# One decoder block on one core: sums on VectorE in two recurrent rounds, another order of the jobs around attention, another place for one expert load, and a shorter end

## The reference

```python
proj = xn @ w_in                      # u | q | k | v | q_idx | k_idx | w_idx | g_ssm | g_att
y_ssm = s5_mixer(u, ...)              # scan of 32 groups x 64 complex states, gelu, GLU
y_att = dsa_attention(q, k, v, q_idx, k_idx, w_idx)   # 64 best keys of 256 by 16 index heads
mixed = g_ssm * (y_ssm @ w_proj_ssm) + g_att * (y_att @ w_proj_attn)
x = x + mixed @ w_out
x = x + moe(rms_norm(x, norm2_g), ...)                # 32 experts of 1024 x 2048 and 1024 x 1024
return rms_norm(x, norm_f_g)
```

## Time and profile before

| | us |
|---|---|
| median of 3 runs | 1153.14 (1152.78 to 1153.84) |
| the profiled execution | 1152.54 |
| its span, first to last instruction | 1150.7 |
| TensorE busy | 1106.9 (96%) |
| VectorE busy | 343.9 (30%) |
| ScalarE busy | 156.4 (14%) |
| DMA, mean over the span | 380 GB/s, 437.73 MB |

### The profile page before, as it was taken

One profiled execution on the slowest core, in us unless ns is written; L12 is line 12 of the kernel. 1 busy time (PEld: TensorE's weight loads), 2 busy tenths in 40 slices (PEclk: granted clock), 3 DMA queues, 4 the chain that ended last, 5 costly groups with the idle time before them and its releaser, 6 DMA issues.

```text
span 1150.7 us, 13804 instructions
## 1 busy us (share of the span) xinstructions
PE 1106.9 (96%) x5566; PEld 484.6 (42%) x5566; DVE 343.9 (30%) x766; ACT 156.4 (14%) x332; POOL 0.7 (0%) x8
## 2 busy tenths in 40 slices
PE   9999999999999999999999999999999999999995
PEld 8878788833333333333333333333333333333331
DVE  7999982122212111111111111211111111111112
ACT  2411461221010000100000000100000000000002
POOL 0000000000000000000000000000000000000000
PEclk9999999999999999999999999999999999999999
DMA  8434576699999999999999999999999999999994
GB/s 337 146 131 154 205 314 272 237 360 429 427 428 428 429 428 429 428 428 429 429 429 428 429 428 428 428 428 428 428 428 428 429 428 428 429 428 428 428 428 207
DMA packets 34010, 437.73 MB, mean 380 GB/s; under 512 B 4032, under 2 KB 4160, under 8 KB 6080
## 3 DMA queue, kind: packets, MB, share of 16 engines
q1 hardware_dynamic: 33696, 436.68, 90.5%
q10 hardware_dynamic: 288, 0.69, 0.2%
HBM read 435.52 MB, written 1.05 MB: 379 GB/s over the span
## 4 chain that ended last, share of the span: by engine, by line
PE 54%; DMA 26%; DVE 6%; SPq 4%; issue 1%; ACT 1%; ACTq 0%
DMA mem<-in_w_moe 26%; PE ps L1327 25%; PE ps L1367 12%; SPq L373 4%; PE ps L1303 3%; PE ps L1286 3%; PE ps L1046 2%; PE ps L1252 2%; DVE mem L601 2%; PE ps L1338 2%; PE ps L1216 1%; PE ps L1294 1%; PE ps L1352 1%; DVE mem L784 1%; DVE xs L601 1%
## 5 line engine op out<-in xcount | busy, mean ns | idle before, releaser
L1327 PE MATMUL ps<-mem,late 128*64 128x512 f32 x2048 | 457.7, 595 | 24.2 <-DMA mem<-in_w_moe 24.2
L1327 PEld LDWEIGHTS ps<-mem,late 128*64 128x64 f32 x2048 | 141.8, 137 | 332.5 <-issue 280.6
L966 DVE TENSOR_SCALAR late<-ps 128x512 f32<-128x512 f32 x32 | 22.1, 692 | 687.4 <-PE ps L1327 687.4
L1367 PE MATMUL ps<-mem,late 128*64 128x512 f32 x1024 | 226.8, 595 | 0.0
L1046 PE MATMUL ps<-mem 128*128 128x256 f32 x640 | 143.5, 382 | 0.0
L1046 PEld LDWEIGHTS ps<-mem 128*128 128x128 f32 x640 | 119.8, 190 | 20.5 <-issue 4.1
L1367 PEld LDWEIGHTS ps<-mem,late 128*64 128x64 f32 x1024 | 70.7, 137 | 133.3 <-issue 128.1
L553 ACT ACTIVATE late<-late 128x512 f32<-128x512 f32 x32 | 20.1, 629 | 513.4 <-DVE late L966 513.4
L1303 PE MATMUL ps<-late 64*128 64x512 f32 x256 | 63.6, 615 | 0.9 <-ACT late L562 0.9
L1286 PE MATMUL ps<-xs,late 128*64 128x512 f32 x256 | 61.9, 604 | 0.8 <-DVE late L601 0.8
L601 DVE TENSOR_TENSOR mem<-mem 128x1024 f32<-128x1024 f32 (+8 forms) x88 | 59.9, 722 | 1.3
(11 more groups left out here) (159 smaller groups left out, 504.3 us busy)
## 6 DMA issues: line engine op xcount, KB each, us to landing
mem<-in_w_moe SPq DMA_DIRECT2D x192, 2048.0 KB, 41.6
mem<-in_w_mix SPq DMA_DIRECT2D x26, 1024.0 KB, 5.7
mem<-in_w_mix SPq DMA_DIRECT2D x2, 512.0 KB, 7.3
out<-xs SPq DMA_DIRECT2D x2, 512.0 KB, 2.9
mem<-mem SPq DMA_DIRECT2D x12, 64.0 KB, 2.7
late<-in_turn_w SPq DMA_DIRECT2D x1, 640.0 KB, 7.5
mem<-in_x_t ACTq DMA_DIRECT2D x1, 512.0 KB, 4.6
mem<-in_x_t SPq DMA_DIRECT2D x1, 512.0 KB, 5.8
```

What stands on the lines that cost most here:

```text
L966: ve.tensor_scalar(gate_z, z[:, 0], LIMIT, None, ALU.min).then_inc(z_gate, 1)
L1327: i = pe.matmul(ps[r, n // 2, :], h_sel[:, k % 4, k // 4, :], w[:, 512 * n:512 * n + 512], start=(k == 0), stop=(k == KD - 1))
L1367: i = pe.matmul(ps[64 * q:64 * q + SLOTS, 2, :], act_tile(k), w[:, 512 * q:512 * q + 512], start=(k == 0), stop=(k == KF - 1))
```

## The change

1. In rounds 0 and 1 (`SUMMED = 2`) VectorE subtracts and adds the four output products in pairs, in place, before `out_ok`; `y_out(0)` and `y_out(1)` then take 8 matmuls each instead of 16.
2. `y_out(0)` stands behind the `VW` job instead of ahead of it.
3. The score jobs begin in the third quarter of `A0` instead of the second quarter of `S3`; `y_out(3)` goes between score jobs 5 and 6.
4. `GLU0` and `GLU1` stand ahead of `logits(1)`, which waits for the first mask (`masked`) and not for its row maximum. `A3` stands ahead of `turn_prob(0)`. `turn_prob(1)` writes to four banks of its own (4 to 7) and no longer to the rotating two.
5. ScalarE's gates, gelu and exponentials are reordered to match; VectorE does `y_ssm` ahead of the rest of `choose_keys(1)`.
6. The tokens are copied straight into `xs` and scaled there in four pieces, `raw` is gone, and so part 5 is loaded together with parts 3 and 8.
7. At the start the two halves of the input and the constant table change queues.
8. The end is rewritten: one sum of squares per token half over 1024 columns, one fused multiplication per half, no tiny matmul.

```diff
-        "A0", "A1", "A2", "GLU0", "GLU1", "P0_0", "P0_1", "A3", "PS0", "PS1", "PS2"] \
-    + [f"P1_{n}" for n in range(4)] + ["PS3"] + [f"W{m}" for m in range(KD)]
+        "A0", "A1", "A2", "GLU0", "GLU1", "A3", "P0_0", "P0_1", "PS0", "PS1", "PS2",
+        "PS3"] + [f"W{m}" for m in range(KD)]
...
-            load_first(3, 8)
+            load_first(3, 5, 8)
...
-            sp.wait_ge(opened, 1)
-            sp.wait_ge(x_norm, TT)
-            load_first(5)
...
-            relus(0, 1)
             gate("S", gate_s, V_BG, 3)
             ac.wait_ge(roped, 3)
-            relus(2, 3, 4, 5)
+            relus(0)
             gate("A", gate_a, V_BG + KD, 0)
-            relus(6, 7)
+            relus(1, 2, 3, 4)
+            gate("A", gate_a, V_BG + KD, 1)
+            relus(5, 6, 7)
...
+            gate("A", gate_a, V_BG + KD, 2)
+            ac.wait_ge(y_raw_ok, 1)
+            ac.activation(y_gelu, y_raw, ACT.Gelu_apprx_tanh).then_inc(gelu_ok, 1)
+            glu_gate(0)
+            ready(ACT.Exp)
+            exponentials(0, 1, 0, NH)
+            glu_gate(1)
+            gate("A", gate_a, V_BG + KD, 3)
+            ready(ACT.Exp)
             prob_turned(0)
...
-            for n, bank_free in enumerate((None, (under_gains, 1), (sum_ok, 1), (under_gains, 3))):
-                if bank_free:
-                    ac.wait_ge(*bank_free)
-                ac.activation(late[:, 512 * n + 512:512 * n + 1024], ps[:, 4 + n, :], ACT.Square,
-                              accum_out=stat[:, 48 + n:49 + n]).then_inc(squared, 1)
-                if n % 2:
-                    t = n // 2
-                    ac.wait_ge(mean_f_ok, t + 1)
-                    ac.activation(stat[:, 4 + t:5 + t], stat[:, t:t + 1], ACT.Sqrt, scale=1.0 / D,
-                                  bias=stat[:, 46:47]).then_inc(root_f_ok, 1)
+            for t in range(TT):
+                if t:
+                    ac.wait_ge(under_gains, 1)
+                ac.activation(late[:, 512 + D * t:512 + D * t + D], ps[:, 4 + 2 * t:6 + 2 * t, :].rearrange("p b c -> p (b c)"),
+                              ACT.Square, accum_out=stat[:, 48 + t:49 + t]).then_inc(squared, 1)
+                ac.wait_ge(squared, t + 1)
+                ac.activation(stat[:, 4 + t:5 + t], stat[:, 48 + t:49 + t], ACT.Sqrt, scale=1.0 / D,
+                              bias=stat[:, 46:47]).then_inc(root_f_ok, 1)
             ac.wait_ge(rstd_f_ok, 2)
-            ac.wait_ge(under_gains, 4)
-            ac.activation(final[:, 1, 0:512], final[:, 1, 0:512], ACT.Copy, scale=stat[:, 7:8]).then_inc(
+            ac.activation(final[:, 1, 512:D], final[:, 1, 512:D], ACT.Copy, scale=stat[:, 7:8]).then_inc(
                 out_ready[1], 1)
...
-                tt(prod_out[3], state_re, ei, ALU.mult).then_inc(out_ok, 1)
+                last = tt(prod_out[3], state_re, ei, ALU.mult)
+                if i < SUMMED:
+                    link(last)
+                    tt(prod_out[0], prod_out[0], prod_out[1], ALU.subtract)
+                    last = tt(prod_out[2], prod_out[2], prod_out[3], ALU.add)
+                last.then_inc(out_ok, 1)
...
-            for n, bank_free in ((1, None), (0, (squared, 1)), (3, (sum_ok, 1)), (2, (squared, 3))):
-                if n == 3:
-                    ve.wait_ge(squared, 2)
-                    tt(stat[:, 0:1], stat[:, 48:49], stat[:, 49:50], ALU.add).then_inc(mean_f_ok, 1)
-                if bank_free:
-                    ve.wait_ge(*bank_free)
-                q = n % 2
-                tt(final[:, n // 2, 512 * q:512 * q + 512], ps[:, 4 + n, :], gfin[:, 512 * q:512 * q + 512],
-                   ALU.mult).then_inc(under_gains, 1)
-            ve.wait_ge(root_f_ok, 1)
-            ve.reciprocal(stat[:, 6:7], stat[:, 4:5]).then_inc(rstd_f_ok, 1)
-            ve.wait_ge(squared, 4)
-            tt(stat[:, 1:2], stat[:, 50:51], stat[:, 51:52], ALU.add).then_inc(mean_f_ok, 1)
-            ve.wait_ge(rstd_f_ok, 1)
-            ve.wait_ge(under_gains, 4)
-            ve.tensor_scalar(final[:, 0, :], final[:, 0, :], stat[:, 6:7], None, ALU.mult).then_inc(out_ready[0], 1)
-            ve.wait_ge(root_f_ok, 2)
-            ve.reciprocal(stat[:, 7:8], stat[:, 5:6]).then_inc(rstd_f_ok, 1)
-            ve.wait_ge(rstd_f_ok, 2)
-            ve.tensor_scalar(final[:, 1, 512:D], final[:, 1, 512:D], stat[:, 7:8], None, ALU.mult).then_inc(
-                out_ready[1], 1)
+            tt(final[:, 1, 512:D], ps[:, 7, :], gfin[:, 512:D], ALU.mult).then_inc(under_gains, 1)
+            for t in range(TT):
+                ve.wait_ge(root_f_ok, t + 1)
+                ve.reciprocal(stat[:, 6 + t:7 + t], stat[:, 4 + t:5 + t]).then_inc(rstd_f_ok, 1)
+                ve.wait_ge(rstd_f_ok, t + 1)
+                w = D if t == 0 else 512
+                ve.scalar_tensor_tensor(final[:, t, 0:w], ps[:, 4 + 2 * t:6 + 2 * t, :].rearrange("p b c -> p (b c)")[:, 0:w],
...
-                for n, c in enumerate((0, 2, 1, 1)):
+                parts = ((0, 0), (1, 2)) if i < SUMMED else ((0, 0), (2, 1), (1, 2), (1, 3))
+                for c, n in parts:
                     for a in range(4):
                         ins = pe.matmul(ps[32 * a:32 * a + 32, 2 + i // 2, (i % 2) * T:(i % 2) * T + T],
                                         c_t[c][:, i, 32 * a:32 * a + 32], prod_out[n][:, a, :],
-                                        start=(n == 0), stop=(n == 3))
+                                        start=(n == 0), stop=(n == parts[-1][1]))
...
             x_job("QI3")
-            y_out(0)
...
             i.then_inc(rot_done, 1)
+            y_out(0)
...
-            x_job("S3", between=scores_from(-1))
-            x_job("A0", between=scores_from(3))
+            x_job("S3")
+            x_job("A0", between=scores_from(-2))
+            x_job("A1", between=scores_from(2))
             y_out(3)
-            x_job("A1", between=scores_from(7))
+            x_job("A2", between=scores_from(6))
             logits(0)
-            x_job("A2")
-            logits(1)
             chunk_arrived(pe, "GLU")
             pe.wait_ge(gelu_ok, 1)
             for n in range(2):
                 feature_job(f"GLU{n}", y_gelu, KS, 2 * n, deep("GLU"))
+            logits(1)
+            x_job("A3")
             pe.wait_ge(tables_in, 16)
             turn_prob(0)
...
-            pe.matmul(ps[0:1, 3, 0:1], ones[0:1, 0:1], ones[0:1, 0:1], start=True, stop=True).then_inc(sum_ok, 1)
```

114 lines of the change are left out of this document (62 added, 52 removed).

## The result

The changed kernel takes 1159.77 us, the median of five executions (1157.72 to 1159.99), against 1153.09 for the kernel before beside it. The ratio is 1.0052, with a 95% interval of 1.0041 to 1.0063: slower by half a per cent, as forecast, by 6.7 us where 4.6 had been forecast. The five times fall in two groups, 1157.7 and 1157.8, and three at 1159.8 to 1160.0. The profiled execution took 1157.81 (span 1156.0), so its trace shows an execution of the lower group; none of the upper group is in it.

What follows compares the result with a forecast made beforehand. Weight DMA limits the expert stage, its start set by the mixing stage (VectorE leads until 150 us, then TensorE). 1152.54 + 6.2 + 0.1 - 0.1 - 1.4 = 1157.3; stated 1157.7, range 1153.6 to 1160.2.

Steps and rivals of the forecast that it cites:

- The sums on VectorE, 4.9: Mixing stage, rounds 0 and 1: the added VectorE operations cost 4.9 us for two rounds, with nothing hiding them.
- the two rivals in which TensorE decides: Mixing stage: TensorE covers the sum up to the scores (1153.2, chance 0.13), or decides all through (1147.9, chance 0.08).
- their own tell-tale, `y_raw` near 143: Start of VectorE's second half: TensorE's work decides all through only if VectorE reaches y_raw by about 143.
- The start, 0.3 gained: First loads: the new order gives back 0.3 us of VectorE's 0.46 us wait for the input.
- The late score jobs: Mixing stage: later score jobs make VectorE wait 3.9 and 2.7 us, reaching y_raw 11.3 late, at 150.3.
- y_raw to the projection: From y_raw to attention's projection: PS0 evicted at 182.6, PS2 starts at 182.7, projection at 193.9, 6.2 us late.
- the lead of 1.8 us: At PS2: TensorE's own list gets there at some 181, 1.8 us ahead of VectorE's release of the bank.
- the delay would still be 4.4: At the projection: with a shorter VectorE chain, TensorE's own waits would take over and leave it 4.4 us late.
- TensorE's clock: Ahead of bu(2): clock may fall in a new wait of about 3 us; up to 3.6 us costs nothing; no chance given.
- Part 5, 0.1: First reload of expert weights: loading part 5 earlier is worth 0.1 us, bounds 0 and 2.1.
- the quick reload: First reload: the stream begins right at its issue, without the 2.1 us start-up, giving 1155.8; chance 0.12.
- The tail, 1.4: End, behind the last input matmuls: the rewritten end gains 1.4 us, bounds 0 and 2.5.

Runs made afterwards that it cites:

- e1: Changed kernel without the sums on VectorE (SUMMED = 0, 16 matmuls in every y_out): 1153.43 us, ratio 1.0005.
- e2: Changed kernel with the first loads on the queues of the kernel before: 1157.37 us, ratio 1.0041.
- e8: Changed kernel with score jobs, y_out(3) and ScalarE's relu copies where the kernel before has them: 1161.48 us, ratio 1.0065.
- e3: Changed kernel with idle matmuls in two TensorE waits, ahead of bu(2) and GLU0: 1158.75 us, ratio 1.0050.
- e5: Changed kernel with idle matmuls in all six long TensorE waits: 1157.87 us, ratio 1.0039.
- e4: Changed kernel with part 5 loaded where the kernel before loads it, behind the scaling of the tokens: 1158.67 us, ratio 1.0049.
- e7: Kernel before with the new end, tokens copied straight into xs, and part 5 early: 1151.24 us, ratio 0.9983.
- e9: Changed kernel without the sums and with the first loads queued as before: 1152.68 us, ratio 0.9995.
- e6: Kernel before with only the sums on VectorE in two rounds and y_out(0), y_out(1) of 8 matmuls: 1159.49 us, ratio 1.0053.
- e10: Kernel before with the new end alone: 1152.15 us, ratio 0.9988.
- e11: Kernel before with new end, direct copies, part 5 early, plus five idle matmuls in each of three waits between router and first expert: 1152.60 us, ratio 0.9994.
- e12: Kernel before with only idle matmuls in the three waits between router and first expert: 1153.37 us, ratio 1.0002.

## Why the prediction was right, and where its steps were not

**The sums on VectorE, 4.9.** Right: 4.88 at `y_raw` and 4.90 at the body between e1 and the changed kernel. Nothing covered them, and the two rivals in which TensorE decides are out; their own tell-tale, `y_raw` near 143, stood at 151.65.

**The start, 0.3 gained.** Wrong, the one step with the wrong sign: it costs 1.0 (e2). The step took the wait for the first half as what counts, and the input's second half on its new queue came 1.73 us late (the row at 9.08). With the forecast's 0.3 of gain that is a shift of 1.3, found again as 1.1 to 1.35 in nearly all marks: 103.5 against 104.64, 134.9 against 136.02, 142.8 against 143.88, 150.3 against 151.65.

**The late score jobs, then y_raw to the projection.** The working was right as a description: waits of 3.83 and 2.14 against 3.9 and 2.7, and from `y_raw` to the eviction of PS0 32.2 us against 32.3. 184.01 for PS2 is the forecast's 182.7 and the 1.3 of the start. But the lead of 1.8 us that TensorE was to have at PS2 wasn't there: it ended `attend` 0.14 after PS0's eviction. 1.5 us of it went into `GLU0`, whose 32 rows took 8.62 at the low clock; without such falls the lead was 1.45 to 1.48. And the sentence that with a shorter VectorE chain "the delay would still be 4.4" was wrong both ways, because TensorE's list is no fixed number. Without the sums (e1) it moves forward with VectorE's, as `bu(2)` and `y_out(2)` wait for VectorE: the projection starts at 189.89, 2.2 late, and VectorE still decides. With the sums in and only the scores earlier (e8) it was 10.5, with the start and the falls of the clock in it.

**TensorE's clock.** This was named as a rival without a chance of its own, with a cover of up to 3.6 us at `bu(2)`. For that place it was right: the fall from 69 to 76 was covered. It is also why the third `y_out` waited 0.33 and not some 2: with `bu(2)`'s wait filled (e3) that wait is 2.11. What the step missed were the other waits. At `GLU0` and PS0 only the lead at PS2 covers a fall, enough for one and not for both, and behind the third `y_out` nothing does (e3's body is 1.8 later than e5's). That the upper group comes from such falls is shown by e5, in which it is gone; at which wait is shown for e3's and e4's executions and not for the changed kernel's own. The profiled execution itself is 0.5 from the sum. The Trainium skill, "TensorE: Matmul & The Clock Gate", section "What's actually happening", says that the clock is halved or full and that when it changes varies from run to run. The traces agree with both: in windows of half a microsecond around the changed kernel's two falls it is 0.50 or 1.00 except in those in which it changes, and the same wait of 1.52 us has a fall behind it in e4 and none in the changed kernel.

**Part 5, 0.1, and the quick reload.** The place of part 5 is worth 0.5 to 1.2 (e4 and the other traces), so the term was small, if not as small as said. The reload issued at 255.92 carried next to nothing up to 257; what had come by 262, (26 + 347) GB/s x 5 us, is 4.35 us at 429 GB/s, so it began at 257.65, 1.7 us after its issue, where 2.1 were taken. The Trainium skill, "DMA: Bandwidth & Descriptors", section "Latency and other measured facts", has about 0.6 to the first byte; that is no statement on the full rate, and the rival built on it is out.

**The tail, 1.4.** It was 1.65, within its bounds, 1.6 of it ahead of the last scaling.

**The sum.** Projection +7.1 (forecast 6.2; the start is 1.3 of it, and 0.4 came back between PS2 and the projection, 10.8 us where 11.2 were taken), to the body 7.4 (with a wait of 0.78 ahead of it, which e7 has too: the copies into `xs`), to the last input matmuls 6.95, tail -1.65: 5.3 in the profiled execution, 4.8 forecast. The median's further 2.0 are the clock, which had no term. The two errors have one sign, and the median stays in the range by 0.4: that it does is in part luck, as nothing in the range stood for the falls of the clock behind `GLU0`, PS0 or the third `y_out`.

What stays open: why one execution's clock falls behind a given wait and another's does not, and at which wait it fell in the changed kernel's own high executions.

## What to carry to other kernels

Before work is moved from one engine to another, read which of the two is full in that stretch: here TensorE's 1.9 us saved went into a wait for VectorE, which paid 4.9 for them. When two engines are near balance, undoing a delay on one only hands the lead to the other (e8); look for the sum over both, and for a third engine whose order ties one to the other, as ScalarE's gate ahead of the gelu does here. And a change that lengthens TensorE's waits is dearer than the waits: the clock may fall behind them, in some executions and not in others, and then a profile of one execution doesn't show the median.

## What the runs showed of the hardware

Behind `bu(2)`'s wait of 3.36 us the granted clock of TensorE was low in all four traces that have it (the changed kernel, e2, e4, e8). Behind the same 2.24 us at `GLU0` it fell in the changed kernel and e4 and not in e1, e2, e8 and e9; behind the same 1.52 us at PS0 it fell in e2, e4 and e8 and not in the changed kernel, e1, e3 and e9. It fell behind 2.11 at the third `y_out` of e3 and behind 1.65 and 1.66 at the first score job of e6 and e8, and not in the kernel before behind 1.64 at `y_out(0)`. A fall at `GLU0` or PS0 cost TensorE 1.5 to 1.7 us on the 32 rows behind it (8.62 to 8.83 against 7.14). At the router, with three waits of 0.8 to 0.95 us between short work, it fell in e10 (0.84 and 0.73 in the windows) and e7 (0.57), and not in the profiled execution of the kernel before. Idle matmuls in the waits narrow the spread of the times to 0.9 us in e5 and 0.8 in e11 and e12, from 2.3, 2.0 and 2.4. They must be shorter than the wait to cost nothing: five of 128x128 in float32 took 1.38 us, and in waits of 0.8 us that put the first expert 1.35 later.
